# Attention outputs of two head groups in one call on column halves, and the sums of Down's weights moved from the mixer into the Down stage

## The reference

```python
h = rms_norm(x, g); z = h @ w_in          # columns: qa ka va | qr kr vr gr | up
ya = sliding_window_attention(qa, ka, va, sinks, rel_bias)   # 6 query heads, 2 key heads, window 128
yr = retention(qr, kr, vr, gr)             # 6 heads, chunks of 128
yp = pool_mixer(up)                        # trailing means over 2, 4, 8, 16 tokens
x = x + concat(ya, yr, yp) @ w_out
x = x + square(relu(rms_norm(x) @ w_up)) @ w_down            # w_up 1024x4096, w_down 4096x1024
out = rms_norm(x, g_final)
```

## Time and profile before

| | |
|---|---|
| time, median of 3 runs | 2230.89 us (2228.69 to 2231.07) |
| profiled execution, its own time | 2232.64 us |
| its span, first to last instruction | 2230.4 us |
| mean granted clock of TensorE | 0.971 |
| busy: PE, PEld | 2089.5 us (94%), 1754.5 us (79%) |
| busy: VectorE, ScalarE, GpSimd | 1334.6 us (60%), 927.4 us (42%), 478.3 us (21%) |
| bytes moved by DMA | 357.61 MB, 160 GB/s |

### The profile page before, as it was taken

The page is one execution under the profiler, slowest core; times in us unless marked ns, Lnnn a source line. Parts: engine busy times, 40 slices in busy tenths (PEclk is TensorE's granted clock), DMA queues, the critical chain, the costliest instruction groups (busy, mean ns, idle before and its releaser), DMA issues.

```text
span 2230.4 us, 28408 instructions
## 1 busy us (share of the span) xinstructions
PE 2089.5 (94%) x10172; PEld 1754.5 (79%) x10172; DVE 1334.6 (60%) x1928; ACT 927.4 (42%) x1581; POOL 478.3 (21%) x387
## 2 busy tenths in 40 slices
PE   8988998889889998879999969999999999999998
PEld 6977797778868886658888858887888888888887
DVE  3447445653575357687777887776654455645456
ACT  4433434344324432454455544444533334433333
POOL 5246523643365326220000120000000000000001
PEclk9989999999999998889999989999999999999999
DMA  7242534343434343225677645557695554854452
GB/s 275 92 143 94 188 102 132 104 167 108 146 105 166 100 148 128 70 81 156 154 175 172 142 109 156 150 151 204 171 327 196 199 200 178 319 226 189 190 197 104
DMA packets 132303, 357.61 MB, mean 160 GB/s; under 512 B 11035, under 2 KB 45628, under 8 KB 117820
## 3 DMA queue, kind: packets, MB, share of 16 engines
q1 hardware_dynamic: 127548, 338.93, 47.8%
q10 hardware_dynamic: 4608, 16.78, 2.0%
HBM read 262.22 MB, written 93.45 MB: 159 GB/s over the span
## 4 chain that ended last, share of the span: by engine, by line
PE 52%; DVE 2%; POOL 1%; issue 1%; ACT 1%; DMA 0%; POOLq 0%; DVEq 0%; ACTq 0%
PE bank L1825 17%; PE bank L1826 17%; PE bank L1827 17%; POOL h_lo L816 1%; DMA wraw<-in_wup 0%; PE bank L2055 0%; DVE h_lo L1439 0%; DVE wt L1591 0%; ACT h_hi L1081 0%; DVE wraw L1591 0%; DVE w_lo L1599 0%; ACT w_hi L1071 0%; DVE hraw L1434 0%; DVE ur L1638 0%; DVE ur L1636 0%
## 5 line engine op out<-in xcount | busy, mean ns | idle before, releaser
L1825 PE MATMUL bank<-h_hi,w_lo 128*128 128x512 f32 x896 | 356.5, 398 | 37.6 <-ACT tA L1098 16.3
L1826 PE MATMUL bank<-h_lo,w_hi 128*128 128x512 f32 x896 | 354.1, 395 | 0.0
L1827 PE MATMUL bank<-h_hi,w_hi 128*128 128x512 f32 x896 | 354.0, 395 | 0.0
L1825 PE MATMUL bank<-d_hi,u_lo 128*128 128x512 f32 x896 | 348.8, 389 | 2.0 <-DVE d_lo L1731 2.0
L1827 PE MATMUL bank<-d_hi,u_hi 128*128 128x512 f32 x896 | 348.6, 389 | 0.0
L1826 PE MATMUL bank<-d_lo,u_hi 128*128 128x512 f32 x896 | 348.6, 389 | 0.0
L686 POOL TENSOR_TENSOR ring_lo<-stage,ring_hi 128x1024 fp32r<-128x1024 f32 x104 | 247.3, 2400 | 315.0 <-ACT ring_hi L848 314.9
L1731 DVE TENSOR_TENSOR u_lo<-u_raw,u_hi 128x1024 fp32r<-128x1024 f32 x112 | 137.1, 1224 | 269.6 <-ACT u_hi L1132 269.6
L1132 ACT ACTIVATE u_hi<-u_raw 128x1024 fp32r<-128x1024 f32 x112 | 118.5, 1058 | 341.7 <-PE bank L1827 327.9
L1825 PE MATMUL bank<-ring_hi,hT_lo 128*128 128x384 f32 (+1 forms) x672 | 248.5, 370 | 0.4 <-DVE hT_lo L1393 0.2
L1827 PE MATMUL bank<-ring_hi,hT_hi 128*128 128x384 f32 (+1 forms) x672 | 237.5, 353 | 0.0
(11 more groups left out here) (185 smaller groups left out, 3495.7 us busy)
## 6 DMA issues: line engine op xcount, KB each, us to landing
u_raw<-u_dram SPq DMA_DIRECT2D x56, 1024.0 KB, 4.8
stage<-in_wmix SPq DMA_DIRECT2D x108, 512.0 KB, 3.7
u_dram<-ur SPq DMA_DIRECT2D x32, 1280.0 KB, 8.5
wraw<-in_wup SPq DMA_DIRECT2D x128, 256.0 KB, 2.9
d_raw<-t_dram SPq DMA_DIRECT2D x32, 1024.0 KB, 6.9
d_raw<-in_wdn SPq DMA_DIRECT2D x24, 1024.0 KB, 8.1
traw<-in_wdn SPq DMA_DIRECT2D x32, 512.0 KB, 3.7
t_dram<-traw SPq DMA_DIRECT2D x32, 512.0 KB, 4.8
```

The source lines that it names most:

```text
L1825: pe.matmul(dst, al, bh, start=(first and k == 0), stop=False, skip_group_check=chain)
L1826: pe.matmul(dst, ah, bl, start=False, stop=False, skip_group_check=chain)
L1827: last = pe.matmul(dst, ah, bh, start=False, stop=(final and k == n - 1), skip_group_check=chain)
```

## The change

Two edits.

**Attention outputs.** `att_out(q, b)` is called once for each block of queries, for both groups, in turns 2, 4 and 6 and after T_UP1. It makes four matmuls instead of two for each group; each has 64 stationary columns, and the output of group g goes to partitions 64 g to 64 g + 63 of `OB`. `yA_high` and `yA_low` handle 128 partitions, once for each block. `evac_pt(i)` waits for the output of the block before.

```diff
-            def att_out(q, i):
-                b, k = i // 2, i % 2
-                pe.wait_ge(pt_evac.sem, pt_evac.now(q, 2 * i + 1))
-                if i:
-                    pe.wait_ge(yAlo_done.sem, yAlo_done.now(q, i - 1))
+            def att_out(q, b):
+                pe.wait_ge(pt_evac.sem, pt_evac.now(q, 4 * b + 3))
+                if b:
+                    pe.wait_ge(yAlo_done.sem, yAlo_done.now(q, b - 1))
...
                 for half in range(2):
-                    last = pe.matmul(OB[:, 0:384], vtok[:, b + half, :], pt[:, k, 384 * half:384 * half + 384],
-                                     start=(half == 0), stop=(half == 1))
+                    for g in range(2):
+                        a = HEAD * g
+                        last = pe.matmul(OB[a:a + HEAD, 0:384], vtok[:, b + half, a:a + HEAD], pt[:, g, 384 * half:384 * half + 384],
+                                         start=(half == 0), stop=(half == 1))
...
                     proj_G(q, 2 * i)
-                    if i:
-                        att_out(q, i - 1)
+                    if i in (2, 4, 6):
+                        att_out(q, i // 2 - 1)
...
                 if i >= 2:
-                    act.wait_ge(o_done.sem, o_done.now(q, i - 2))
+                    act.wait_ge(o_done.sem, o_done.now(q, i // 2 - 1))
...
-                act.activation(yA_hi[a:a + HEAD, :, b * P:(b + 1) * P],
-                               OB[a:a + HEAD, 0:384].rearrange("p (c t) -> p c t", c=3), ACT.Copy).then_inc(yAhi_done.sem, 1)
+                act.activation(yA_hi[:, :, b * P:(b + 1) * P],
+                               OB[:, 0:384].rearrange("p (c t) -> p c t", c=3), ACT.Copy).then_inc(yAhi_done.sem, 1)
```

```diff
+        E_FROM = {0: B12, 4: B12, 6: B22}
+        E_STEPS = [s for s in range(STEPS) if s // GP % NK in E_FROM]
+        DSUM_STEPS = [s for s in range(STEPS) if s // GP % NK in (0, 2, 3, 4, 6)]
...
                 if s >= RAW:
                     sp.wait_ge(m_lo_done, 4 * (s - RAW) + 4)
-                if k in (0, 1, 5):
-                    src = wdn[g, D_FROM[k]].rearrange("p (j n) -> p j n", j=GP)
-                else:
-                    src = t_dram[g, D_FROM[k]]
-                sp.dma_start(d_raw[s % RAW][:, :, :], src).then_inc(d_full[s % RAW], 16)
+                    if s - RAW in DSUM_STEPS:
+                        sp.wait_ge(dsum_done, dsum_at(s - RAW, 1))
+                sp.dma_start(d_raw[s % RAW][:, :, :], wdn[g, D_FROM[k]].rearrange("p (j n) -> p j n", j=GP)).then_inc(d_full[s % RAW], 16)
+
+            def load_step_e(s):
+                p, k, g = step_of(s)
+                i = E_STEPS.index(s)
+                if i >= RAW:
+                    sp.wait_ge(dsum_done, dsum_at(E_STEPS[i - RAW], 1))
+                sp.dma_start(e_raw[i % RAW][:, :, :], wdn[g, E_FROM[k]].rearrange("p (j n) -> p j n", j=GP)).then_inc(e_full[i % RAW], 16)
...
             sp.wait_ge(prod_done, end)
+            load_step_e(2)
             for t in range(TB):
                 load_top(0, t)
-            for t in range(TB):
-                load_low(0, t)
...
+                    src, hi, full = d_block(s), d_hi, d_full[s % RAW]
+                    if s // GP % NK in (2, 3, 4, 6):
+                        act.wait_ge(dsum_done, dsum_at(s, h))
...
+            def down_sum(s):
...
+                if k == 0:
+                    dst, a, b = kept, e, d
...
+                elif k == 2:
+                    dst, a, b = kept, d, kept
...
+                elif k == 3:
+                    dst, a, b = d, d, kept
...
+                else:
+                    dst, a, b = d, e, d
+                for h in range(2):
+                    rows = slice(2 * h, 2 * h + 2)
+                    dve.tensor_tensor(dst[:, rows, :], a[:, rows, :], b[:, rows, :], ALU.subtract).then_inc(dsum_done, 1)
...
             combine_end(PAIRS - 1)
             m_low(0, 2)
             m_low(0, 3)
+            down_sum(0)
             for part in range(4):
                 m_low(1, part)
+            down_sum(1)
+            down_sum(2)
             for s in range(STEPS):
...
                 if s + 2 < STEPS:
                     for part in range(4):
                         m_low(s + 2, part)
+                if s + 3 in DSUM_STEPS:
+                    down_sum(s + 3)
```

More of the change, by code:

```diff
@@ L160, in build @@
         gch = work("gch", 90368, [P, 3 * P])
-        traw = [work(f"traw{s}", 179200 + 4096 * s, [P, 4, 256]) for s in range(2)]
         R = work("R", 91904, [P, 3 * P])
@@ L219, in build @@
         ur = work("ur", 210944, [P, 6, HALF])
-        u_raw = [work(f"u_raw{s}", a, [P, GP, HALF]) for s, a in enumerate((0, 16384, 32768))]
+        u_raw = [work(f"u_raw{s}", a, [P, GP, HALF]) for s, a in enumerate((0, 16384, 118784))]
         d_raw = [work(f"d_raw{s}", a, [P, GP, 512]) for s, a in enumerate((8192, 24576, 110592))]
+        e_raw = [work(f"e_raw{s}", a, [P, GP, 512]) for s, a in enumerate((32768, 126976, 155648))]
         u_hi = work("u_hi", 45056, [P, 8, HALF], F32R)
@@ L227, in build @@
         d_lo = work("d_lo", 94208, [P, 8, 512], F32R)
[L228 to L231, removed]
+        top = work("top", 135168, [P, TB, D])
+        t_keep = [work(f"t_keep{g}", 188416 - 8192 * g, [P, GP, 512]) for g in range(GP)]
+        low = work("low", 196608, [P, TB, D])
+        zacc = work("zacc", 212992, [P, TB, 512])
+        sqj = work("sqj", 221184, [P, D], mybir.dt.bfloat16)
         bank = [ps(f"bank{i}") for i in range(8)]
@@ L438, in _ @@
         def _(sp):
-            for e in [tab_full, *x_full, *st_full, *traw_full, *t_stored]:
+            for e in [tab_full, *x_full, *st_full]:
                 sp.sem_inc(e.sem, e.primed)
@@ L615, in _ @@
                     load_step_d(1)
+                if n == 30:
+                    load_step_e(0)
             end = NK * PAIRS
             sp.wait_ge(prod_done, end - 2)
-            load_step(2)
+            load_step_u(2)
+            load_step_d(2)
+            sp.wait_ge(prod_done, end - 1)
+            load_step_e(1)
             store_u(PAIRS - 1)
@@ L644, in _ @@
                 p, w = divmod(s, NK * GP)
+                if s == 4:
+                    sp.wait_ge(ua_stored[0], 8 * PAIRS)
+                    sp.wait_ge(ua_stored[1], 8 * PAIRS)
+                    sp.wait_ge(ub_stored, 16 * PAIRS)
+                    sp.wait_ge(ur_stored, 16 * PAIRS)
+                    for t in range(TB):
+                        load_low(0, t)
                 if w == 26:
@@ L1123, in m_high @@
                 else:
-                    src, hi, full = d_raw[s % RAW], d_hi, d_full[s % RAW]
+                    src, hi, full = d_block(s), d_hi, d_full[s % RAW]
+                    if s // GP % NK in (2, 3, 4, 6):
+                        act.wait_ge(dsum_done, dsum_at(s, h))
                 act.wait_ge(full, 16 * (s // RAW + 1))
@@ L1726, in m_low @@
                 cell = slice(4 * (s % 2) + 2 * h, 4 * (s % 2) + 2 * h + 2)
-                src, hi, lo = (u_raw[s % RAW], u_hi, u_lo) if part % 2 == 0 else (d_raw[s % RAW], d_hi, d_lo)
+                src, hi, lo = (u_raw[s % RAW], u_hi, u_lo) if part % 2 == 0 else (d_block(s), d_hi, d_lo)
                 dve.wait_ge(m_hi_done, 4 * s + part + 1)
```

109 lines of the change are left out of this document (46 added, 63 removed).

## The result

| kernel | median | executions | ratio to before, 95% interval |
|---|---|---|---|
| before | 2230.98 us | 2228.69 to 2232.15 | |
| after | 2159.43 us | 2158.43 to 2160.71 | 0.9681 [0.9664, 0.9698] |

The change makes the kernel 3.2% faster, 71.6 us by the medians. The profiled execution of after takes 2158.43 us, with a span of 2156.2 us, 74.2 us less than the span of before.

What follows compares the result with a forecast made beforehand. TensorE was taken to idle in the mixer, waiting for scores behind VectorE's weight sums and their loads. -39.2 - 16.1 + 1 - 17 + 1.5 = -69.8 us gave 2162.8, less 1.75 for the median 2161 us; 8-in-10 range 2150 to 2186.

Steps and rivals of the forecast that it cites:

- Term 1: Mixer: with the weight sums gone, TensorE's waits for normalised scores (-39.2 us) and the half clock behind them (-16.1) go.
- third rival: Mixer: waits for the scores are only partly the sums', another chain is late by itself; 2181 us, chance 0.08.
- +1 us for the output part: Mixer, output part of the quarters: 0.25 us lost in each, having less cover; an estimate with bounds 0 and 11 us.
- Term 2: Attention outputs: 16 calls on column halves replace 32 on the whole array, 1.71 us against 2.78; -17 us.
- two run at a time with one slot of stagger: Attention outputs: pattern read from row halves, by which eight records take five slots, 1.71 us a call.
- first rival: Attention outputs: the column halves don't run together; 2178 us, chance 0.17.
- the second: Attention outputs: weight loads of the other column half don't slip under a running matmul; 2199 us, chance 0.04.
- Term 3: Down: 80 subtractions of 1.14 us on VectorE and 24 third loads stay hidden, except +1.5 us at the start.
- wait at step 3: Start of Down: late loads and VectorE's sum ahead of the low parts hold TensorE up by +1.5 us.
- slow-transfer rival: Down: transfers don't get beyond some 200 GB/s, so three-block steps take 15.8 us; 2279 us, chance 0.03.
- lead at the group changes: Down: VectorE works over one step ahead, hiding the sums; the rival without it costs 32 us, 2193, chance 0.08.

Runs made afterwards that it cites:

- sums part alone: Kernel before with the sums of Down's weights moved into Down, each output call still on the whole array: 2181.37 us, ratio 0.9769.
- one pair later: Kernel before with the sums on each quarter's seventh half made one turn later, ahead of the eighth's, all still in the mixer: 2211.73 us, ratio 0.9901.

## Why the prediction was right

The forecast was 2161 us, and 2159.43 came. Its sum, -69.8 us against the profiled execution, stands beside -74.2. By the timed runs terms 1 and 3 together gave 1.3 us less than forecast and term 2 some 3 us more, so a part of the closeness is two errors that cancel.

**Term 1 (-54.3) held.** The waits at the transposes went whole and the turns run at full clock. The run with the sums part alone has this term and that of Down, -52.8 by my steps, and measured -51.5. That both waits would go, and no second chain would be late behind them, is what its list of waits shows. The third rival (waits only partly the sums') is out. The last turn's scaling beside GpSimd is slow (3.13 us), but it ends at 136.6 and TensorE asks at 140.9. The +1 us for the output part can't be told apart: mixer -73.9, less term 1's -55.3 and the halves' -21.3, leaves +2.7 us, and five traces of the same mixer are 869.5 to 873.6 us long.

**Term 2 (-17) had the mechanism right and the size 4 us short.** The call takes 1.45 us and not 1.71: 16 x 1.33 = 21 us, the lower bound of -22 almost. The step that failed is "two run at a time with one slot of stagger". In the single records of the row halves (L1961) the two of a pair start 7 ns apart, at 84.355 and 84.362, and the next pair at 84.569; after that it is 0.11 us from pair to pair. What I had read as a stagger is a first slot of 0.21 us. The trace of before already had it (L1939 at 74.486, 74.492, 74.699). The column halves do the same: 82.914 and 82.921, then 83.288, 83.610, 83.933, four slots and no fifth, and the change to the row halves is in the last one (0.42 us instead of 0.32). The first rival (halves don't run together) is out, as is the second: the weight loads of both halves slip under running matmuls, in the pairs shown above. The Trainium skill, TensorE: Matmul & The Clock Gate, Part 3, says that a weight load overlaps running matmuls only when the row group differs; here it doesn't differ, and they overlap. The prediction said that the trace of before can't judge this rule; it could, since the loads of L1967 lie hidden there on the full array, with one row group. The same part says that matmuls start in program order, and the run with exchanged loops, beside that with a wait, speaks against it.

**Term 3 (+1.5, hidden otherwise) held.** Down is 2.7 us longer, of which 2.3 are the wait at step 3 that the prediction placed there, behind the late `u_raw` and the sum in front of the low parts; without the 2.1 MB of `top` ahead of them it is gone. VectorE has 68%. The third load never bounds: no wait of VectorE names `e_raw`, the window moves 249 GB/s and 366 from 1820 to 1840, and the 2279 us of the slow-transfer rival needed a limit of 200. The lead at the group changes is real; twice the sums use it up around the turn of the passes.

**Not in the sum:** Up became 3.0 us shorter without an edit there. The trace's clock records put 131.1 us of the run before at half clock and 76.7 of the run after. Four other kernels with the same mixer and the same Up have 89.3 to 103.1 us, and their Up is 664.6 to 669.5 us long, so a few us of any single trace are this scatter and no effect of an edit. By the medians the change is worth 71.6 us and not the 74.2 of the two traces.

## What to carry to other kernels

A wait on an in-order engine is priced by what is queued behind it, and it hides other gains: 21 us of TensorE work were worth 10.7 while the transfers set the pace and 20 when they no longer did, so clear the wait first, then judge the rest. When such work is in the way, the cheap tries are to issue its transfers earlier and to consume them a turn later. Here the earlier issue alone brought 28 us, the later use of one pair alone 22, of some 55; both together, with all pairs used later, brought as much as moving the work away. All pairs used later with the old points of issue was not tried. Before a fast block is costed from a first start and a last end, look at the single records, since a slow first slot and a stagger look the same from outside.

## What the hardware showed unexpectedly

- Matmuls of two column halves run side by side in both program orders that were tried: exchanging the loops changed the distance within a pair from 7 to 13 ns and the call not at all (1.45 us), and only a wait parted them (3.00 us).
- A subtraction of 128 x 256 on VectorE takes 0.42 us, and 1.53 to 2.64 us when it lies wholly beside work of GpSimd (13 subtractions of the run with one pair later, against 128 without overlap in before).
- The time at half clock differs by up to 26 us between single executions of five kernels with the same mixer and Up (76.7 to 103.1 us), some 13 us of run time at most. It goes with the spread of one kernel's executions too: with the rows of the residual loaded later, the slowest of five (2164.99 us) has a mean granted clock of 0.977 and the fastest (2155.27 us) 0.983. What sets it off in one execution and not in another stays open.
